# A two-layer decoder trunk in fp32: the down projections by a Winograd form of Strassen's algorithm, with weight sums on GpSimd

## The chip, the cores and the metric

The kernel runs on one core of a Trainium2 chip. Five engines work side by side, each in its own program order: TensorE (PE, matmuls), VectorE (DVE), ScalarE (ACT), GpSimd (POOL) and SyncE (SP, which issues DMAs). They meet only through semaphores. SBUF is the memory on the core, PSUM holds the sums of the matmuls in 8 banks of 128 partitions x 512 fp32, and DRAM is outside the core. The metric is the device time of one execution in microseconds.

## The reference, cut to what matters

There are 256 tokens, a model width of 2048, and two layers. Each layer is a mixer (sliding-window attention in layer 0, forgetting attention in layer 1) and then a SwiGLU network with 5632 hidden columns. All is fp32.

```
for i in range(DEPTH):                       # DEPTH = 2
    h = rmsnorm(x, g[0])
    y = attention(h)                         # two kinds
    x = x + rmsnorm(y, g[1])
    h = rmsnorm(x, g[2])
    gu = h @ w_gate_up                       # 2048 x 11264
    y = (silu(gate) * up) @ w_down           # 5632 x 2048: the down projection
    x = x + rmsnorm(y, g[3])
```

## The kernel before, in words

**Products in three parts.** TensorE takes the values in a rounded fp32 format (F32R), so each operand is split into a high part (the rounded value) and a low part (the rest). A product is three matmuls: high x high, high x low, low x high (`product`, L1336 to L1340). Each is 128x128 weights (the tokens' block) against 128x512 of the weight matrix, summed in a PSUM bank.

**The weights' way.** SP loads pairs of 128x512 weight tiles into `stage` (8 tiles). ACT rounds a tile into `ring_hi` (`round_tile`, L594 to L607), DVE writes the rest, `stage` minus `ring_hi`, into `ring_lo` (`rest_tile`, L808 to L817). Both rings have 24 tiles. Where the norm's gain is folded in (gate, up, q, k, v) ACT scales, and DVE uses a scalar_tensor_tensor (L817), else a tensor_tensor (L815).

**Units and steps.** The program is a row of units of 16 weight tiles. A unit has 32 steps: a step is one product, 3 matmuls, and each tile is used for both token blocks (t = 0, 1). While PE works through a unit, ACT and DVE prepare the next unit's tiles, one every second step. In what order each engine does its other work is written out by step numbers in tables at the top of the file.

**The SwiGLU network** works in 11 groups of 512 hidden columns. A group has three units: gate, up, down. After the up unit DVE makes `h_sb` = silu(gate) * up (L1061), turns it into `h_t` by 32x32 transposes (L1087, 32 instructions in a group), ACT rounds `h_t` into `h_hi` (L752), DVE makes `h_lo` (L1069). The down unit multiplies it with a 512 x 2048 block of `w_down`: 16 tiles x 2 token blocks = 32 products, 96 matmuls. After each of the 8 output chunks (2 token blocks x 4 column chunks) DVE adds the bank to `y_sb` in SBUF (`add_y`, L1106; L1103 copies in the first group). The residual `x_sb` (16 KB in each partition) lies in SBUF all the time. POOL does nothing in this network but a few small operations on the norms at its ends, and the load of the norm's gains.

**POOL's work elsewhere.** In the sliding-window layer POOL does the rotary embedding (L1220 to L1226: tensor_tensor of 128x64 and 128x128); in the forgetting layer it adds the mask to the bias (L1265, L1267: tensor_tensor 128x128, L1266: copy) and issues DMAs.

Of the kernel before, what the change touches and what calls it, by code (L numbers as in the profile page):

```python
# [7 lines left out]
F32 = mybir.dt.float32  # L8
# [35 lines left out]
LT = LOOP_UNITS * UT  # L44
# [6 lines left out]
U_FOX = U_FFN[0] + 3 * FG  # L51
U_FOX_OUT = U_FOX + FOX_UNITS
U_FFN[1] = U_FOX_OUT + NC_D
U_END = U_FFN[1] + 3 * FG
# [45 lines left out]
HIDDEN_TURNED = {(1, 17): (0, 0), (1, 19): (0, 1), (2, 1): (1, 0), (2, 3): (1, 1)}  # L100
HIDDEN_HI = {(1, 25): 0, (2, 5): 1}
HIDDEN_LO = {(1, 23): 0, (2, 5): 1}
# [32 lines left out]
def step_order(s, first=False):  # L135

    if first:
        return s // 4 % 2, s // 8 * 4 + s % 4
    return s // UT, s % UT

# [22 lines left out]
def build(nc, x, positions, norm_gains, swa_w_in, swa_sinks, swa_w_out,  # L163
          fox_w_in, fox_b_f, fox_w_out, ffn_w_gate_up, ffn_w_down, out):
    with ExitStack() as ctx:
# [40 lines left out]
        arena = sb("arena", [P, 51 * 1024 // 4])  # L206
# [22 lines left out]
        diag = at("diag", 40 * KB, [P, P])  # L229
        ssq_end = at("ssq_end", 41 * KB, [P, NC_D + 1])  # L230
# [18 lines left out]
        x_ps = [bank[b] for b in (6, 7, 4, 5)]  # L249

# [20 lines left out]
        x_sum = sem("x_sum")  # L271
        x_squared, pre_mean, pre_rstd = sem("x_squared"), sem("pre_mean"), sem("pre_rstd")
# [12 lines left out]

        cum_dram = nc.dram_tensor("cum_scratch", (NH, SEQ), F32, kind="Internal").ap()
# [4 lines left out]
        def weights(u, i, pr):  # L291
# [16 lines left out]
            if u < U_FOX or u >= U_FFN[1]:  # L308
                layer = 0 if u < U_FOX else 1
                g, part = divmod(u - U_FFN[layer], 3)  # L310
                g = g + i
                if part < 2:
                    return cols(ffn_w_gate_up[layer], g * CH + part * D_FF)
# [14 lines left out]
        def gain_row(u):  # L328

            if u < U_SWA_OUT:  # L330
                return 0
            if U_FOX <= u < U_FOX_OUT:
                return 4
            for layer in range(2):
                if U_FFN[layer] <= u < U_FFN[layer] + 3 * FG and (u - U_FFN[layer]) % 3 < 2:
                    return 4 * layer + 2
            return None
# [28 lines left out]

        def whole_program(loop, unit):

            def looped(u, n):
                with loop(n) as i:  # L370
                    for part in range(LOOP_UNITS):
# [6 lines left out]
            straight(U_SWA, U_FFN[0] + 3)  # L378
            looped(U_FFN[0] + 3, FG - 2)
            straight(U_FOX - 3, U_FOX + 3)  # L380
            looped(U_FOX + 3, NG - 2)
            straight(U_FOX_OUT - 3, U_FFN[1] + 3)
            looped(U_FFN[1] + 3, FG - 2)
            straight(U_END - 3, U_END)

        def ffn_part(u):

            for layer in range(2):
                if U_FFN[layer] <= u < U_FFN[layer] + 3 * FG:
                    return (layer, *divmod(u - U_FFN[layer], 3))  # L390
            return None
# [95 lines left out]
        def wait_transposed(eng, layer, g, i, t):  # L487
            if turned_on_pe(g, t):
                eng.wait_ge(ht_last, layer + 1)
            else:  # L490
                eng.wait_ge(ht_done, 2 * (layer * FG + g) - layer + t + 1 + 2 * i)

        def wait_swept(eng, u, i, t, n=0):
# [5 lines left out]
            elif t == 1:  # L499
                eng.wait_ge(tile_used, UT * u + (4 * (n + 1) if ffn and ffn[2] == 2 else UT) + LT * i)  # L500
            elif ffn is None:
                eng.wait_ge(proj_done, mixer_unit(u) + 1 + LOOP_UNITS * i)
            elif ffn[2] < 2:
                eng.wait_ge((gate_done, up_done)[ffn[2]], ffn[0] * FG + ffn[1] + 1 + i)
            else:
                eng.wait_ge(down_done, NC_D * (ffn[0] * FG + ffn[1]) + n + 1 + NC_D * i)
# [7 lines left out]
        def y_gain_count(b, t, q):  # L514

            k = NT * q + t if b % 2 else NC_D * t + q
            return 8 * (b - 1) + k + 1

# [6 lines left out]
        def _(sp):  # L525
# [26 lines left out]

            def unit(u, i):
                for pr in range(UT // PAIR):
                    if u == 0 and pr != 1:
# [3 lines left out]
                    if pair >= NSTAGE:  # L559

                        sp.wait_ge(raw_loaded[slot], 16)
                        sp.wait_ge(lo_ready, PAIR * (pair - NSTAGE + 1) + LT * i)
# [28 lines left out]
        def _(act):  # L591
            act.dma_start(gains_in[:, :], norm_gains.rearrange("l g (k p) -> (l g k) p", p=P)).then_inc(gains_loaded, 16)

            def round_tile(u, i, j):  # L594
# [3 lines left out]
                if j % PAIR == 0:  # L598
                    act.wait_ge(raw_loaded[pair % NSTAGE], loads_before(pair) + 16 * LT // STAGE * i)
                if n >= RING:  # L600
                    act.wait_ge(tile_used, n - RING + 1 + LT * i)
                row = gain_row(u)
                src = stage[:, n % STAGE, :]
                if row is None:
                    nc.scalar.activation(ring_hi[:, n % RING, :], src, ACT.Identity).then_inc(hi_ready, 1)  # L605
                else:
                    nc.scalar.activation(ring_hi[:, n % RING, :], src, ACT.Identity,  # L607
                                         scale=g_t[:, row * KT + j:row * KT + j + 1]).then_inc(hi_ready, 1)

# [92 lines left out]
            def unit(u, i):  # L702
                ffn = ffn_part(u)
                for s in range(STEPS):
# [33 lines left out]
                    if ffn:  # L738
                        layer, g, part = ffn
                        f = layer * FG + g  # L740
                        if part == 1 and s in (0, 2):
# [28 lines left out]
                    if s % 2 == 0 and u + 1 < U_END:  # L770
                        round_tile(u + 1, i, s // 2)

            def squares_of_y(b, t, n):

                f = (b // 2) * FG - 1
# [18 lines left out]
            for h in range(2):  # L794
                act.wait_ge(y_added, 8 * 2 * FG + h)
# [11 lines left out]
        def _(dve):  # L807
            def rest_tile(u, i, j):  # L808

                n = u * UT + j  # L810
                dve.wait_ge(hi_ready, n + 1 + LT * i)
                row = gain_row(u)
                src, hi, lo = stage[:, n % STAGE, :], ring_hi[:, n % RING, :].bitcast(F32), ring_lo[:, n % RING, :]
                if row is None:
                    nc.vector.tensor_tensor(lo, src, hi, ALU.subtract).then_inc(lo_ready, 1)  # L815
                else:
                    nc.vector.scalar_tensor_tensor(out=lo, in0=src, scalar=g_t[:, row * KT + j:row * KT + j + 1], in1=hi,  # L817
                                                   op0=ALU.mult, op1=ALU.subtract).then_inc(lo_ready, 1)

# [35 lines left out]
            def residual_sum(b, t, q):  # L855

                if q == 0:
                    dve.wait_ge(post_rstd, 2 * (b - 1) + t + 1)
                dve.wait_ge(y_gained, y_gain_count(b, t, q))
# [133 lines left out]
            def unit(u, i):  # L993
                ffn = ffn_part(u)
                for s in range(STEPS):
# [57 lines left out]
                    if ffn:  # L1053
                        layer, g, part = ffn
                        f = layer * FG + g
                        if (part, s) in ((1, 17), (2, 1)):

                            t = 0 if part == 1 else 1
                            dve.wait_ge(gate_read, 2 * f + t + 1 + 2 * i)
                            wait_swept(dve, u if part == 1 else u - 1, i, t)  # L1060
                            nc.vector.scalar_tensor_tensor(out=h_sb[:, t, :], in0=main[2 + t][:, :], scalar=pre_r[:, t:t + 1],  # L1061
                                                           in1=h_sb[:, t, :], op0=ALU.mult, op1=ALU.mult).then_inc(hidden, 1)
                        if (part, s) in HIDDEN_TURNED and not turned_on_pe(g, HIDDEN_TURNED[part, s][0]):
                            turn_hidden(layer, g, i, *HIDDEN_TURNED[part, s])
# [26 lines left out]
            def add_y(u, f, i, g, k):  # L1091
# [496 lines left out]
```

## Time and profile before

| | |
|---|---|
| median of 3 timed runs | 2106.15 us (2105.09 to 2106.24) |
| profiled execution, first to last instruction | 2104.5 us |
| PE, busy share of the span | 100% |
| DVE | 77% |
| ACT | 55% |
| POOL | 7% |

The profile page gives the profiled execution by its span alone. Matmuls overlap in the pipeline, so PE's busy time is a union: that PE is busy all the time doesn't say how close its matmuls follow. The number of matmuls in a stretch does. A group of instructions is a source line with an operation and the names of what it writes and reads; "busy, mean ns" is the sum and the mean duration of one, and a duration includes what the instruction waits for on its own data path once it has started.

### The profile page before, as it was taken

To read this page: it belongs to the slowest core of one execution; us is meant where nothing else is said; L and a number is where in the kernel's file an instruction comes from. 1 tells how busy PE (TensorE), PEld (TensorE's weight loads), DVE (VectorE), ACT (ScalarE), POOL (GpSimd) and SP (SyncE) were. 2 spreads that over 40 slices of the span, in tenths; PEclk is the share of its full clock that TensorE was granted. 3 is DMA by queue.
4 is the path that set the end of the run, shared out by engine and by line. 5 is a ranking of instruction groups with operands and counts; after the bars stand their busy time and mean duration, and the time that the engine had idled before them with its cause. 6 is when DMAs were issued, how large, how long until landed. Compare 5 with 4: busy or idle time off the path is not lost.

```text
span 2104.5 us, 32177 instructions
## 1 busy us (share of the span) xinstructions
PE 2094.2 (100%) x9603; PEld 1718.9 (82%) x9603; DVE 1615.4 (77%) x3299; ACT 1152.9 (55%) x2061; POOL 156.6 (7%) x311
## 2 busy tenths in 40 slices
PE   9999999999999999999999999999999999999998
PEld 7877888888888888888888887888888888888886
DVE  6798677887667776678898898577877668776686
ACT  7666565544455454555666555665544545445553
POOL 2110000000000000000152343000000000000000
PEclk9999999999999999999999999999999999999999
DMA  7699866665666655665687787756555665556662
GB/s 257 211 247 253 223 206 206 195 191 173 199 199 199 197 171 190 199 204 161 202 247 219 214 251 215 234 190 216 189 187 178 199 217 184 188 178 203 206 193 87
DMA packets 221564, 425.01 MB, mean 202 GB/s; under 512 B 15808, under 2 KB 25440, under 8 KB 220976
## 3 DMA queue, kind: packets, MB, share of 16 engines
q1 hardware_dynamic: 214528, 402.45, 61.6%
q0 software_dynamic: 6672, 21.31, 3.7%
q8 instruction: 37, 0.61, 0.1%
q10 hardware_dynamic: 288, 0.33, 0.1%
q14 instruction: 39, 0.32, 0.1%
HBM read 409.31 MB, written 14.71 MB: 201 GB/s over the span
## 4 chain that ended last, share of the span: by engine, by line
PE 97%; DMA 1%; issue 1%; SPq 1%; ACT 0%; POOL 0%; DVE 0%; POOLq 0%
PE bank L1338 31%; PE bank L1340 31%; PE bank L1339 31%; PE bank L1385 1%; PE bank L1410 1%; PE bank L1351 1%; DMA x_sb<-x 0%; DMA p_f<-first_scratch 0%; DMA stage<-swa_w_out 0%; PE bank L1368 0%; SPq L541 0%; SPq L566 0%; PE bank L1432 0%; PE bank L1429 0%; PE bank L1571 0%
## 5 line engine op out<-in xcount | busy, mean ns | idle before, releaser
L1338 PE MATMUL bank<-ring_hi,a_hi 128*128 128x512 f32 x2240 | 880.3, 393 | 0.5 <-DVE ring_lo L817 0.5
L1340 PE MATMUL bank<-ring_hi,a_lo 128*128 128x512 f32 x2240 | 873.1, 390 | 0.0
L1339 PE MATMUL bank<-ring_lo,a_hi 128*128 128x512 f32 x2240 | 872.8, 390 | 0.0
L607 ACT ACTIVATE ring_hi<-stage,g_t 128x512 fp32r<-128x512 f32 x992 | 661.2, 717 | 376.6 <-DMA stage<-ffn_w_gate_up 203.0
L817 DVE SCALAR_TENSOR_TENSOR ring_lo<-stage,g_t,ring_hi 128x512 fp32r<-128x512 f32 x992 | 708.5, 759 | 147.3 <-ACT ring_hi L607 144.9
L1338 PEld LDWEIGHTS bank<-ring_hi,a_hi 128*128 128x128 f32 x2240 | 420.9, 188 | 92.9 <-issue 5.9
L1340 PEld LDWEIGHTS bank<-ring_hi,a_lo 128*128 128x128 f32 x2240 | 420.8, 188 | 88.1
L1339 PEld LDWEIGHTS bank<-ring_lo,a_hi 128*128 128x128 f32 x2240 | 421.1, 188 | 84.7
L815 DVE TENSOR_TENSOR ring_lo<-stage,ring_hi 128x512 fp32r<-128x512 f32 x480 | 305.5, 687 | 139.9 <-ACT ring_hi L605 138.5
L605 ACT ACTIVATE ring_hi<-stage 128x512 fp32r<-128x512 f32 x480 | 278.4, 624 | 225.0 <-PE bank L1340 149.5
L1338 PE MATMUL bank<-ring_hi,h_hi 128*128 128x512 f32 x704 | 274.6, 390 | 0.0
L1340 PE MATMUL bank<-ring_hi,h_lo 128*128 128x512 f32 x704 | 274.2, 389 | 0.0
L1339 PE MATMUL bank<-ring_lo,h_hi 128*128 128x512 f32 x704 | 274.2, 389 | 0.0
L1087 DVE STREAM_TRANSPOSE h_t<-h_sb 32x128 f32<-32x128 f32 x672 | 203.5, 303 | 10.8
L1340 PEld LDWEIGHTS bank<-ring_hi,h_lo 128*128 128x128 f32 x704 | 132.2, 188 | 27.4
L1338 PEld LDWEIGHTS bank<-ring_hi,h_hi 128*128 128x128 f32 x704 | 132.3, 188 | 27.2
L1339 PEld LDWEIGHTS bank<-ring_lo,h_hi 128*128 128x128 f32 x704 | 132.3, 188 | 27.1
L1205 POOL TENSOR_TENSOR post_r<-post_ms,half_pow 128x1 f32<-128x1 f32 x8 | 7.6, 948 | 1491.6 <-DVE post_ms L844 1491.6
L1106 DVE TENSOR_TENSOR y_sb<-bank,y_sb 128x512 f32<-128x512 f32 x159 | 109.5, 688 | 11.6 <-PE bank L1340 10.8
L1061 DVE SCALAR_TENSOR_TENSOR h_sb<-bank,pre_r,h_sb 128x512 f32<-128x512 f32 x44 | 33.0, 749 | 108.8 <-PE bank L1340 108.8
L752 ACT ACTIVATE h_hi<-h_t 128x512 fp32r<-128x512 f32 x42 | 26.6, 633 | 125.7 <-DVE h_t L1087 125.7
L667 ACT ACTIVATE prob<-prob,neg_mx 128x129 f32<-128x129 f32 (+3 forms) x128 | 56.9, 447 | 39.6 <-DVE neg_mx L933 39.3
(148 smaller groups left out, 836.6 us busy)
## 6 DMA issues: line engine op xcount, KB each, us to landing
stage<-ffn_w_gate_up SPq DMA_DIRECT2D x352, 512.0 KB, 4.6
stage<-ffn_w_down SPq DMA_DIRECT2D x176, 512.0 KB, 5.5
stage<-fox_w_in SPq DMA_DIRECT2D x96, 512.0 KB, 4.7
stage<-swa_w_in SPq DMA_DIRECT2D x48, 512.0 KB, 4.7
stage<-swa_w_out SPq DMA_DIRECT2D x64, 256.0 KB, 6.2
stage<-fox_w_out SPq DMA_DIRECT2D x32, 512.0 KB, 5.5
first_scratch<-first_blocks SPq DMA_DIRECT2D x16, 384.0 KB, 5.4
p_f<-first_scratch SPq DMA_DIRECT2D x64, 96.0 KB, 3.9
```

Source lines behind the costliest of these rows:

```text
L605: nc.scalar.activation(ring_hi[:, n % RING, :], src, ACT.Identity).then_inc(hi_ready, 1)
L607: nc.scalar.activation(ring_hi[:, n % RING, :], src, ACT.Identity, scale=g_t[:, row * KT + j:row * KT + j + 1]).then_inc(hi_ready, 1)
L667: last = nc.scalar.activation(prob[:, b, cols], prob[:, b, cols], ACT.Exp, bias=neg_mx[:, j, t:t + 1], accum_out=den[:, j, t:t + 1])
L752: nc.scalar.activation(h_hi[:, :, tok(t)], hidden_transposed(g, t), ACT.Identity).then_inc(ht_hi, 1)
L815: nc.vector.tensor_tensor(lo, src, hi, ALU.subtract).then_inc(lo_ready, 1)
L817: nc.vector.scalar_tensor_tensor(out=lo, in0=src, scalar=g_t[:, row * KT + j:row * KT + j + 1], in1=hi, op0=ALU.mult, op1=ALU.subtract).th ...
L1061: nc.vector.scalar_tensor_tensor(out=h_sb[:, t, :], in0=main[2 + t][:, :], scalar=pre_r[:, t:t + 1], in1=h_sb[:, t, :], op0=ALU.mult, op1= ...
L1087: last = nc.vector.transpose(h_t[Q * b:Q * (b + 1), :, P * t + Q * a:P * t + Q * (a + 1)], src)
L1106: nc.vector.tensor_tensor(dst, main[n][:, :], dst, ALU.add).then_inc(y_added, 1)
L1338: nc.tensor.matmul(dst, hi_a, hi_w, start=start, stop=False)
L1339: nc.tensor.matmul(dst, hi_a, lo_w, start=False, stop=False)
L1340: return nc.tensor.matmul(dst, lo_a, hi_w, start=False, stop=stop)
```

## The change

All down products but those of the last of the 11 groups of a layer are computed by the Winograd form of Strassen's algorithm. The product of a group (256 tokens x 512) with half of its down block (512 x 1024) is cut into 2x2 blocks (128 tokens x 256, and 256 x 512) and takes 7 block products in place of 8. A block product is two weight tiles side by side, 6 matmuls. There are 20 such halves in a layer.

- The down units of these ten groups are gone. Their 7 block products (`down_pair`) are spread over the gate and the up unit of the next group, at steps 17, 19, 21, 23, 25, 27, 31 (gate) and 4, 8, ... 28 (up). A group thus has two units of 96 + 42 matmuls. In the first group of a layer the gate and the up unit are as before, and after the last group's up unit comes its down unit as before.
- The weight sums are made on POOL, four tensor_tensor of 128 x 1024 for a half (`sum_weights`), and two of the seven rests (T1, T4) as well. The other five rests are DVE's (`rest_pair`, 128 x 1024). ACT rounds all seven (`round_pair`). The sums of the hidden blocks are four tensor_tensor of 128 x 256 on POOL for a group (`sum_hidden`); ACT rounds them, DVE makes their rests (`sum_rests`).
- DVE adds each of the 7 products to `y_sb` from its bank (`add_pair`, 128x512), 14 in a group. Transposes are over both token blocks at once (`turn_group`, 16 of 32x256 in a group), the rest of the hidden block is one of 128x1024 (`hidden_rests`).
- The down weights are loaded into the place of `x_sb` (`down_w`, one buffer of 128 x 8 x 512). `x_sb` is stored to DRAM before the first half of a layer, and loaded back after the last (`save_x`, `load_x`, on POOL's queue).
- The ring has 16 fixed places for tiles and 4 x 2 for the block products' pairs. In the units with block products t changes every 4 steps (`step_order`).

```diff
+FFN_UNITS = 2 * FG + 1
...
-U_FOX = U_FFN[0] + 3 * FG
+U_FOX = U_FFN[0] + FFN_UNITS
+NPROD = 7
+B11, B21, T1, T2, B22, T3, T4 = range(NPROD)
+POOL_LO = (T1, T4)
+PRODUCT_STEPS = ((17, 19, 21, 23, 25, 27, 31), (4, 8, 12, 16, 20, 24, 28))
+PAIR_HI = ({18: (0, 4), 20: (0, 5), 22: (0, 6), 25: (1, 0), 27: (1, 1), 29: (1, 2)},
+           {0: (0, 3), 6: (0, 4), 10: (0, 5), 14: (0, 6), 18: (1, 0), 22: (1, 1), 26: (1, 2), 30: (1, 3)})
...
+            def load_down(u, i, second):
+                if q % NP_LAYER == 0:
+                    sp.wait_ge(x_saved, 16 * (layer + 1))
...
+            def round_pair(u, i, k):
+                wait_place(act, ("pair", p), i, u)
+                nc.scalar.activation(ring_hi[:, PLACE["pair", p]:PLACE["pair", p] + 2, :], pair_source(k), ACT.Identity).then_inc(pair_hi, 1)
...
+            def rest_pair(u, i, k):
+                dve.wait_ge(pair_hi, p + 1 + 4 * NPROD * i)
+                nc.vector.tensor_tensor(ring_lo[:, both, :], pair_source(k), ring_hi[:, both, :].bitcast(F32), ALU.subtract).then_inc(pair_lo, 1)
...
+            def add_pair(u, i, k):
+                nc.vector.tensor_tensor(dst, ps[:, :], dst, ALU.add).then_inc(pair_added, 1)
...
+            def sum_weights(q, i):
+                wait_loaded(0)
+                if q > 0:
+                    wait_rested(T4, q - 1)
+                nc.gpsimd.tensor_tensor(sums[0][:, :, :], b11, b12, ALU.add).then_inc(sums_made, 1)
+                wait_loaded(2)
+                pool.wait_ge(pair_lo, rested + DVE_LO.index(B11) + 1)
+                nc.gpsimd.tensor_tensor(sums[1][:, :, :], b22, b12, ALU.add).then_inc(sums_made, 1)
+                pool.wait_ge(sums_made, made + 1)
+                nc.gpsimd.tensor_tensor(sums[2][:, :, :], sums[0][:, :, :], b22, ALU.add).then_inc(sums_made, 1)
+                rest(T1)
+                pool.wait_ge(sums_made, made + 3)
+                wait_rested(T1, q)
+                nc.gpsimd.tensor_tensor(sums[0][:, :, :], sums[2][:, :, :], b21, ALU.add).then_inc(sums_made, 1)
+                if q % 2 == 0:
+                    sum_hidden(q, i)
+                rest(T4)
...
+            def down_pair(u, i, k):
+                for r in range(2):
+                    last = product(ps[:, :], a_h, a_l, ring_hi[:, slot, :], ring_lo[:, slot, :], k < 3 and r == 0, r == 1, True)
+                last.then_inc(pair_done, 1)
```

## Rows read from the trace of the kernel before

**Rows 1.** The page's first part: busy time and instructions of each engine.
```profile
PE 2094.2 (100%) x9603; PEld 1718.9 (82%) x9603; DVE 1615.4 (77%) x3299; ACT 1152.9 (55%) x2061; POOL 156.6 (7%) x311
```

**Rows 2.** Busy time by window: PE, PEld, DVE, ACT, POOL; clock, DMA share, GB/s.
```profile
300.00:365.28 65.28, 65.28 (x290) 54.10 (x289) 49.14 (x92) 32.84 (x52) 0.00 (x0) 1.00 0.62 198
2084.00:2104.40 20.40, 14.20 (x56) 10.03 (x54) 12.41 (x24) 4.80 (x14) 1.89 (x2) 0.88 0.29 103
```

**Rows 3.** Timeline of ACT, one instruction of three groups in turn: start, duration.
```profile
355.30 0.69 ACT L747 ACTIVATE h_sb<-bank,pre_r 128x512 f32<-128x512 f32 x1 [3.27 <-PE bank L1340]
420.57 0.69 ACT L747 ACTIVATE h_sb<-bank,pre_r 128x512 f32<-128x512 f32 x1 [3.38 <-PE bank L1340]
485.86 0.69 ACT L747 ACTIVATE h_sb<-bank,pre_r 128x512 f32<-128x512 f32 x1 [3.35 <-PE bank L1340]
```

**Rows 4.** The page's groups: count | busy, mean ns | idle before, releaser.
```profile
L1338 PE MATMUL bank<-ring_hi,h_hi 128*128 128x512 f32 x704 | 274.6, 390 | 0.0
L605 ACT ACTIVATE ring_hi<-stage 128x512 fp32r<-128x512 f32 x480 | 278.4, 624 | 225.0 <-PE bank L1340 149.5
```

**Rows 5.** Groups of DVE between 300 and 1000 us (the SwiGLU network of layer 0).
```profile
L817 DVE SCALAR_TENSOR_TENSOR ring_lo<-stage,g_t,ring_hi 128x512 fp32r<-128x512 f32 x339 | 238.5, 749 | 54.3 <-ACT ring_hi L607 54.0
L815 DVE TENSOR_TENSOR ring_lo<-stage,ring_hi 128x512 fp32r<-128x512 f32 x168 | 105.9, 687 | 45.9 <-ACT ring_hi L605 45.4
L1087 DVE STREAM_TRANSPOSE h_t<-h_sb 32x128 f32<-32x128 f32 x336 | 101.8, 303 | 5.4
L1106 DVE TENSOR_TENSOR y_sb<-bank,y_sb 128x512 f32<-128x512 f32 x80 | 55.1, 689 | 5.3 <-PE bank L1340 5.0
L1061 DVE SCALAR_TENSOR_TENSOR h_sb<-bank,pre_r,h_sb 128x512 f32<-128x512 f32 x22 | 16.5, 749 | 54.3 <-PE bank L1340 54.3
L1069 DVE TENSOR_TENSOR h_lo<-h_t,h_hi 128x512 fp32r<-128x512 f32 x21 | 14.4, 684 | 0.0
```

**Rows 6.** Groups of DVE over the whole span, two other shapes.
```profile
L877 DVE STREAM_TRANSPOSE k_t<-stg 32x256 f32<-32x256 f32 x64 | 27.9, 436 | 1.0
L952 DVE TENSOR_TENSOR a_lo<-bank,a_hi 128x256 fp32r<-128x256 f32 x8 | 3.0, 419 | 4.6 <-ACT a_hi L690 4.6
```

**Rows 7.** Single lines: duration in ns min/median/max, first and last start.
```profile
L1265 POOL TENSOR_TENSOR prob<-cum_b,mask x32: 456/474/1000, 1047.1 to 1288.0; 128x128 f32<-128x128 f32 x32
L1220 POOL TENSOR_TENSOR rope_tmp<-stg,rope_s x10: 322/362/875, 34.2 to 166.4; 128x64 f32<-128x64 f32 x10
L620 ACT ACTIVATE y_sb<-x_sb x6: 1907/1908/1909, 278.4 to 1393.4; 128x2048 f32<-128x2048 f32 x6
L928 DVE CUSTOM_DVE_ANT_0 prob<-bank,prob x64: 279/353/423, 1051.1 to 1301.0; 128x128 f32<-128x128 f32 x32, 128x256 f32<-128x256 f32 x32
```

**Rows 8.** Timeline 1280 to 1290 us, DVE, then POOL (first and last of six).
```profile
1285.94 0.38 DVE L952 TENSOR_TENSOR a_lo<-o_t,a_hi 128x256 fp32r<-128x256 f32 x1
1286.84 2.53 DVE L952 TENSOR_TENSOR a_lo<-o_t,a_hi 128x256 fp32r<-128x256 f32 x1
...
1286.91 0.48 POOL L1265 TENSOR_TENSOR prob<-cum_b,mask 128x128 f32<-128x128 f32 x1
...
1288.64 0.45 POOL L1267 TENSOR_TENSOR prob<-cum_b,mask 128x128 f32<-128x128 f32 x1
```

**Rows 9.** Timeline 34 to 40 us: DVE, and one of POOL's in it.
```profile
34.73 5.71 DVE L817 SCALAR_TENSOR_TENSOR ring_lo<-stage,g_t,ring_hi 128x512 fp32r<-128x512 f32 x7 [0.29 <-ACT ring_hi L607]
...
38.22 0.79 POOL L1224 TENSOR_TENSOR stg<-stg,rope_c 128x128 f32<-128x128 f32 x1
```

**Rows 10.** Timeline 1090 to 1110 us, DVE: POOL busy at first, idle at last.
```profile
1097.83 3.02 DVE L817 SCALAR_TENSOR_TENSOR ring_lo<-stage,g_t,ring_hi 128x512 fp32r<-128x512 f32 x3
...
1102.70 1.41 DVE L817 SCALAR_TENSOR_TENSOR ring_lo<-stage,g_t,ring_hi 128x512 fp32r<-128x512 f32 x2
```

**Rows 11.** Timeline of ACT: the squares of x at the start of the network.
```profile
284.40 1.91 ACT L620 ACTIVATE y_sb<-x_sb 128x2048 f32<-128x2048 f32 x1
```

More of the change, by code:

```diff
@@ L132, with ffn_index, pair_unit, pair_number @@
 OUT_GAIN = {84: (0, 0), 88: (1, 0), 92: (0, 1), 98: (1, 1), 102: (0, 2), 106: (1, 2)}
-def step_order(s, first=False):
-    if first:
+def ffn_index(u):
+    for layer in range(2):
+        if U_FFN[layer] <= u < U_FFN[layer] + FFN_UNITS:
+            return layer, u - U_FFN[layer]
+    return None
+def pair_unit(u):
+    f = ffn_index(u)
+    return f is not None and 2 <= f[1] < 2 * FG
+def pair_number(u):
+    layer, n = ffn_index(u)
+    return NP_LAYER * layer + n - 2
+def in_fours(u):
+    f = ffn_index(u)
+    return f is not None and 1 <= f[1] < 2 * FG - 1
@@ new lines, in pairs_rounded, with ring_places @@
+def pairs_rounded(u, s):
+    f = ffn_index(u)
+    if f is None or f[1] == 0 or s not in PAIR_HI[f[1] % 2]:
+        return []
+    later, k = PAIR_HI[f[1] % 2][s]
+    return [(u + later, k)] if pair_unit(u + later) else []
+def ring_places():
+    place, before, last = {}, {}, {}
+    n = 0
+    for u in range(U_END):
+        f = ffn_index(u)
+        fixed = f is not None and f[1] >= 2
+        if fixed and f[1] == 2:
+            first = n % RING
+        for j in range(UT):
+            slot = (first + j) % RING if fixed else n % RING
+            if not fixed:
+                n += 1
+            place[u, j] = slot
+            before[u, j] = last.get(slot)
+            last[slot] = ("tile", u * UT + j)
+        if pair_unit(u):
+            for k in range(NPROD):
+                p = NPROD * pair_number(u) + k
+                slot = (first + UT + 2 * (p % 4)) % RING
+                place["pair", p] = slot
+                before["pair", p] = last[slot + 1]
+                last[slot] = last[slot + 1] = ("pair", p)
+        if fixed and f[1] == 2 * FG:
+            n = first + UT
+    return place, before
@@ new lines, in turn_group @@
+            def turn_group(u, i, a):
+                layer, g, _ = ffn_part(u)
+                if a == 0:
+                    dve.wait_ge(hidden, 2 * (layer * FG + g - 1) + 2 + 4 * i)
+                    if pair_number(u) >= 2:
+                        dve.wait_ge(s_made, 2 * pair_number(u) + 8 * i)
+                for b in range(P // Q):
+                    src = h_sb[Q * a:Q * (a + 1), :, :].rearrange("p t (k b j) -> p t k b j", k=4, j=Q)[:, :, :, b, :]
+                    dst = h_t[Q * b:Q * (b + 1), :, :].rearrange("p k (t a i) -> p t k a i", t=NT, i=Q)[:, :, :, a, :]
+                    last = nc.vector.transpose(dst, src)
+                if a == P // Q - 1:
+                    last.then_inc(ht_done, 1)
@@ L1517, in unit @@
                     n_k = 4 if down else KT
[L1518 removed]
+                    last = product(dst[:, :], a_h[:, k, tok(t)], a_l[:, k, tok(t)], ring_hi[:, PLACE[tile], :], ring_lo[:, PLACE[tile], :],
                                    k == 0, k == n_k - 1)
```

386 lines of the change are left out of this document (306 added, 80 removed).

## The prediction

> **What bounds the kernel now.** I read the page's busy shares first, then the windows of the SwiGLU network, then DVE's groups in it, and last the timeline wherever DVE and POOL run together. The shares [rows 1] say PE 100%, DVE 77%, ACT 55%, POOL 7%. In the network the same instruction comes back every 65.28 us (420.57 - 355.30 = 65.27, 485.86 - 420.57 = 65.29) [rows 3]: that is one group. A group holds 288 product matmuls, so PE issues one every 65.28 / 288 = 226.7 ns; the 390 ns of one [rows 4] overlap. In that window PE is busy for all 65.28 us at clock 1.00, DVE for 49.14, ACT for 32.84, POOL for none [rows 2]. DVE's idle time there ends with ACT's rounding or with PE's bank [rows 5]: both follow PE. So PE sets the pace, and DVE has 16.1 us of slack in a group. The network is 2 x 11 groups of the kernel, the change touches 20 of them.
>
> **PE's part.** A group had 96 down matmuls and gets 2 x 7 x 6 = 84. That is 12 x 226.7 ns = 2.72 us less, a group of 62.56 us if PE stays the bound, and 20 x 2.72 = 54.4 us in all. Nothing on PE is added.
>
> **DVE's own work in a group**, by durations of rows 5 and 6:
> - rests of gate and up tiles: 32 x 0.749 = 24.0 us, as before.
> - rests of block products: 10 of 128x1024. No such size is in the trace. 256 columns take 0.419 [rows 6] and 512 take 0.687 [rows 5], so 1.05 ns a column and 1.22 us for 1024: 12.2 us, for 16 x 0.687 = 11.0 before. The bounds are 0.687 (if further columns were free) and 1.37 (twice 0.687).
> - additions to y: 14 x 0.689 = 9.6 us, for 8 x 0.689 = 5.5.
> - silu x up: 2 x 0.749 = 1.5, as before.
> - transposes: 16 of 32x256 at 0.436 = 7.0, for 32 x 0.303 = 9.7.
> - rest of the hidden block 1.22, and rests of its sums 2 x 0.687 = 1.4; before 2 x 0.684 = 1.4.
>
> This sums to 56.9 us, for 53.1 before. The 53.1 show as 49.14 busy [rows 2], because neighbours overlap by 4.0 us over 92 instructions, 0.043 each; 77 instructions give 3.3, so DVE needs 53.6 us of the 62.56. ACT rounds 14 pairs of 128x1024 in place of 16 tiles: with 0.624 for 512 [rows 4] and 1.91 for 2048 [rows 7], 0.84 ns a column, a pair is 1.05 us and 14 are 14.8 for 10.0 before; with the sums' rounding ACT stays near 40 us. SP's loads are the same bytes. By these alone PE would still be the bound.
>
> **POOL's work in a group**, which is new: 12 tensor_tensor of 128x1024 and 4 of 128x256. Rows 7 have 128 columns at 0.456 at the least (median 0.474) and 64 at 0.322, so 2.2 ns a column. Then 1024 columns take 0.46 + 896 x 0.0022 = 2.43 us, 256 take 0.74, and a group 12 x 2.43 + 4 x 0.74 = 32.1 us. Bounds for one of 1024: 0.46 (if columns were free) and 8 x 0.474 = 3.8. I take 2.43, since two rows give the slope. POOL has the time for it in 62.56 us. The Trainium skill, page "GPSIMD Engine Reference", section 3.1, has a tensor_tensor of 2048 fp32 columns at 4497 ns, an estimate of about 2.3 us for 1024; no row here shows either size.
>
> **What POOL does to DVE** is the term that decides. At 1286.84 a DVE tensor_tensor of 256 columns with both inputs in SBUF takes 2.53 us, where its neighbour takes 0.38. Beside it lie six POOL instructions without a gap, from 1286.91 to 1288.64 + 0.45 = 1289.09, which is 2.18 us, all at their undisturbed durations [rows 8]. DVE lost 2.53 - 0.42 = 2.11 us of these 2.18: it waited for all of them. Three rests take 3.02 us beside POOL's, where two alone take 1.41 [rows 10], so three would take 2.08. The wait goes both ways: POOL's 128-column tensor_tensor takes 0.79 beside DVE's rests [rows 9], and up to 1.00 [rows 7]. DVE's operations with one input in PSUM show none of it: L928 ranges from 0.279 to 0.423 over two shapes, also beside POOL's [rows 7]. The Trainium skill, page "SBUF — State Buffer", section "Who interferes with whom", has this as a rule: a DVE instruction with two SBUF inputs contends with a GpSimd instruction that reads SBUF, and whoever has the shared port keeps it for the whole instruction. By that rule, the trace agrees: 2.11 of 2.18 us. It speaks against this change, whose gain was worked out above as if the engines were free of each other.
>
> Of DVE's 56.9 us, those with two SBUF inputs are 24.0 + 12.2 + 1.2 + 1.4 = 38.8 us. Only the additions, transposes and silu x up, 18.1 us, can run while POOL computes. DVE works in order, and after nearly each addition (0.689) comes a rest. The transposes, 7 us in one stretch (steps 2 to 8 of the gate unit), lie where POOL waits for their result or has at most one operation. So of a POOL operation of 2.43 us DVE hides a fraction of one addition and stands still for the rest. Bounds of DVE's loss: the share of rows 8, 97% of 32.1 = 31 us; and the share of rows 9, where seven rests take 5.71 us for 0.75 + 6 x 0.66 = 4.7 undisturbed [rows 10], so 1.0 us lost beside seven small POOL operations of some 2.8 us, 35%, that is 11 us. Long operations are nearer to rows 8, because what isn't lost in rows 9 is the fixed part of a short one. With 18.1 of 56.9 us free of the port I take 78%: 25 us. Then DVE needs 53.6 + 25 = 78.6 us in a group, more than PE's 62.56 and than the 65.28 of before. DVE is the bound, and PE waits for `ring_lo`. The slack that costs nothing now is 62.56 - 53.6 = 9 us; from a loss of 65.28 - 53.6 = 11.7 us on (36% of POOL's time) the kernel is slower than before.
>
> 20 x (78.6 - 65.28) = +266 us.
>
> **Waits at the ends.** The store of x waits for the squares, which end at 284.40 + 1.91 = 286.3 [rows 11]. It moves 2.1 MB, 10.6 us at 198 GB/s [rows 2] beside the weights, and the first down block, as large, comes behind it, at about 308. ACT asks for it at step 18 of the first up unit, about 289 + 18 x 0.68 = 301, and what is queued behind it on ACT are the next unit's tiles from the seventh on, and behind these DVE's rests and PE. With six tiles ready PE can go on for some 8 us. I take 2.5 us for a layer, from 0 to 10, 5 in all. SP stands still meanwhile too, but `stage` holds 8 tiles. The way back, x and the gains (3 MB, about 16 us), is asked for after the last rests, about step 18 of the last up unit; x is wanted at step 17 of the down unit, some 26 us later: hidden.
>
> **Sum.** Span 2104.5 + 266 + 5 = 2375.5; the timed median lies 1.65 us above this span, so 2377 us.
>
> **Rivals.**
> 1. *PE stays the bound.* POOL's operations fall into DVE's slack, or the long ones hold DVE for less than the short ones suggest: 2106.15 - 54.4 + 5 = 2057 us. For it: 9 us of slack, and rows 9 with 35%. Against it: 38.8 - 2 us of DVE and even 26 us of POOL on one port are 63 us in a group of 62.56, before any order is looked at. It decides from a loss under 9 us. Chance 0.14, and 0.03 for what comes out between it and no change, 0.03 for no change.
> 2. *DVE is the bound but hides half:* a loss of 16 us, a group of 69.6 us, +86 + 5: 2197 us. For it: POOL's operations wait for each other's semaphores and for ACT, and let DVE in between. Chance 0.15.
> 3. *PE's clock falls as well.* At the end PE is busy 14.2 of 20.4 us and the granted clock is 0.88 of 2.4 GHz, so part of it was at 1.2 [rows 2]. If PE's gaps did that in a quarter of the groups, each would take 2 x 62.56 = 125 us: 5 x (125 - 78.6) = +232, 2609 us. Against it: DVE's stops are some 2.4 us, between bursts of matmuls, and PE would be busy 80%. Chance 0.04.
>
> **Numbers.** The forecast has 0.61. Its own range is a loss of 19 to 31 us: 72.6 to 84.7 us a group, 2258 to 2500. The range that holds 8 in 10 leaves out rival 1 and the far ends, and takes in rival 2: 2130 to 2480. What a measurement of this kernel tells from no change is about 0.2%, 4 us. Faster 0.17, same 0.03, slower 0.80.
>
> **What would show it.** The period of a group in the windows: near 79 us, PE busy about 80%, DVE over 95%. DVE's rests (L817's successor) with a mean well above 0.749, and `rest_pair`'s above 1.22 and up to 3.6, while the additions stay at 0.69 and the transposes at 0.44. POOL's operations of 1024 columns at 2.4 us at the least, and often longer. PE's idle time released by `ring_lo`. It would be wrong if the period is near 62.6, or if the rests keep their durations beside POOL's, or if PE waits for POOL's sums instead.

## The result, and the profile after

The changed kernel takes 2344.3 us (median of 4 runs, 2342.72 to 2344.4) for 2105.93 of the kernel before: a ratio of 1.113, 95% interval 1.1115 to 1.1146. The forecast was 2377. The span is 2342.6 us, 238.1 more than before, where 271 were forecast.

First the page of the changed kernel: busy time of each engine, then groups (count | busy, mean ns | idle before, releaser). They answer to [rows 1, 4, 5].

```profile
PE 2130.2 (91%) x9363; PEld 1720.3 (73%) x9363; DVE 2094.3 (89%) x2999; ACT 1264.3 (54%) x2041; POOL 916.3 (39%) x635
...
L1694 PE MATMUL bank<-ring_hi,h_hi 128*128 128x512 f32 x304 | 141.2, 465 | 198.9 <-DVE y_sb L1083 149.7
L1034 DVE TENSOR_TENSOR ring_lo<-down_w,ring_hi 128x1024 fp32r<-128x1024 f32 x120 | 254.3, 2119 | 1.8 <-ACT ring_hi L793 1.7
```

PE has 240 matmuls less and is no longer busy all the time; DVE has 300 instructions less and is busy for 479 us more. The windows of the SwiGLU network (columns as in [rows 2]), first 550 us, then one group of it:

```profile
400.00:950.00 550.00, 483.66 (x2000) 390.95 (x1999) 527.50 (x565) 274.72 (x366) 270.51 (x116) 0.95 0.51 165
584.37:660.19 75.82, 66.63 (x278) 53.85 (x277) 73.54 (x78) 38.57 (x53) 38.03 (x17) 0.95 0.52 166
```

DVE is busy 96% of the time, PE 88%, POOL 49%. The bound has moved from PE to DVE. The period is again that of one ACT instruction, the silu of a gate tile, in the timeline of ACT; it answers to [rows 3]:

```profile
507.23 0.66 ACT L946 ACTIVATE h_sb<-bank,pre_r 128x512 f32<-128x512 f32 x1
...
584.37 0.66 ACT L946 ACTIVATE h_sb<-bank,pre_r 128x512 f32<-128x512 f32 x1
...
660.19 0.67 ACT L946 ACTIVATE h_sb<-bank,pre_r 128x512 f32<-128x512 f32 x1
```

77.14 and 75.82 us; over the four periods from 507.23 to 813.05 the mean is 76.5, and over the 18 inner periods of both layers 76.2, for 65.28 before. (A layer has 10 periods from its first silu to that of its last group; the first one is counted apart below.) What has grown is in the groups of DVE between 400 and 950 us, which answer to [rows 5]:

```profile
L1024 DVE SCALAR_TENSOR_TENSOR ring_lo<-stage,g_t,ring_hi 128x512 fp32r<-128x512 f32 x230 | 274.2, 1209 | 2.7 <-ACT ring_hi L780 2.5
L1034 DVE TENSOR_TENSOR ring_lo<-down_w,ring_hi 128x1024 fp32r<-128x1024 f32 x42 | 89.0, 2119 | 0.0
L1046 DVE STREAM_TRANSPOSE h_t<-h_sb 32x256 f32<-32x256 f32 x128 | 55.8, 436 | 3.0
L1085 DVE TENSOR_TENSOR y_sb<-bank,y_sb 128x512 f32<-128x512 f32 x70 | 47.6, 681 | 7.5 <-PE bank L1696 7.2
L1034 DVE TENSOR_TENSOR ring_lo<-sums,ring_hi 128x1024 fp32r<-128x1024 f32 x29 | 35.1, 1210 | 0.0
...
L1054 DVE TENSOR_TENSOR h_lo<-h_t,h_hi 128x1024 fp32r<-128x1024 f32 x8 | 12.4, 1548 | 9.3 <-ACT h_hi L802 9.3
```

The rests of gate and up tiles take 1.209 us in place of 0.749, the rests of `down_w` 2.119 where the same instruction on `sums` takes 1.210. These are means of two kinds, told apart by the start and end of each instruction in the trace: the 107 of the 230 rests of L1024 that lie beside a POOL operation take 1.748 us, the other 123 take 0.740; of the rests of `down_w`, 21 lie beside one and take 3.026, 21 don't and take 1.211. None of the 29 rests of `sums` lies beside one. Additions (one input in PSUM) stay at 0.68, also the 28 of L1083, all of which lie beside POOL operations. No transpose does in this window; they are put to the test in experiment 5. POOL in the same window:

```profile
L1590 POOL TENSOR_TENSOR ring_lo<-sums,ring_hi 128x1024 fp32r<-128x1024 f32 x28 | 79.2, 2829 | 140.7 <-ACT ring_hi L793 140.7
L1601 POOL TENSOR_TENSOR sums<-sums,down_w 128x1024 f32<-128x1024 f32 x14 | 43.3, 3090 | 0.0
```

The timeline shows how it happens. DVE first, then POOL, same stretch (start, duration):

```profile
582.93 2.83 DVE L1034 TENSOR_TENSOR ring_lo<-down_w,ring_hi 128x1024 fp32r<-128x1024 f32 x1
585.69 2.82 DVE L1024 SCALAR_TENSOR_TENSOR ring_lo<-stage,g_t,ring_hi 128x512 fp32r<-128x512 f32 x1
588.43 0.67 DVE L1083 TENSOR_TENSOR y_sb<-y_sb,bank 128x512 f32<-128x512 f32 x1
589.03 2.25 DVE L1024 SCALAR_TENSOR_TENSOR ring_lo<-stage,g_t,ring_hi 128x512 fp32r<-128x512 f32 x1
...
595.13 3.39 DVE L1024 SCALAR_TENSOR_TENSOR ring_lo<-stage,g_t,ring_hi 128x512 fp32r<-128x512 f32 x5
```

```profile
581.83 2.85 POOL L1599 TENSOR_TENSOR sums<-down_w 128x1024 f32<-128x1024 f32 x1 [1.16 <-DVE ring_lo L1034]
584.64 3.32 POOL L1601 TENSOR_TENSOR sums<-sums,down_w 128x1024 f32<-128x1024 f32 x1
587.92 2.81 POOL L1590 TENSOR_TENSOR ring_lo<-sums,ring_hi 128x1024 fp32r<-128x1024 f32 x1
590.81 2.71 POOL L1605 TENSOR_TENSOR sums<-sums,down_w 128x1024 f32<-128x1024 f32 x1
...
606.52 2.47 POOL L1590 TENSOR_TENSOR ring_lo<-sums,ring_hi 128x1024 fp32r<-128x1024 f32 x1 [12.99 <-ACT ring_hi L793]
```

Four POOL operations stand nearly back to back from 581.83 to 593.52. In them DVE gets through about one rest for each of POOL's: the rest that starts at 585.69 ends at 588.51, just behind POOL's end at 587.96. The addition in between takes its usual 0.67. Once POOL is done, at 595.13, five rests take 3.39 us together. The loss is mutual: POOL's 1024 columns take 2.47 us with little beside them (2.39 at the least, at 302.20 us, with DVE idle) and 2.7 to 3.3 here.

### The profile page after: what moved, and what is told of

It is laid out like the page before. It is cut to its first block and busy times, and to the rows that moved or that the text cites. A ratio compares the mean times of both kernels' runs of the same rounds, so it can differ in the third digit from the quotient of the medians.

```text
span 2342.6 us, 32002 instructions
## 1 busy us (share of the span) xinstructions
PE 2130.2 (91%) x9363; PEld 1720.3 (73%) x9363; DVE 2094.3 (89%) x2999; ACT 1264.3 (54%) x2041; POOL 916.3 (39%) x635
## 5 line engine op out<-in xcount | busy, mean ns | idle before, releaser
L1024 DVE SCALAR_TENSOR_TENSOR ring_lo<-stage,g_t,ring_hi 128x512 fp32r<-128x512 f32 x992 | 1020.1, 1054 | 72.7 <-ACT ring_hi L780 70.8
L1590 POOL TENSOR_TENSOR ring_lo<-sums,ring_hi 128x1024 fp32r<-128x1024 f32 x80 | 225.9, 2824 | 407.3 <-ACT ring_hi L793 407.3
L793 ACT ACTIVATE ring_hi<-sums 128x1024 fp32r<-128x1024 f32 x160 | 169.9, 1062 | 352.9 <-PE bank L1696 352.3
L1694 PE MATMUL bank<-ring_hi,h_hi 128*128 128x512 f32 x304 | 141.2, 465 | 198.9 <-DVE y_sb L1083 149.7
L1034 DVE TENSOR_TENSOR ring_lo<-down_w,ring_hi 128x1024 fp32r<-128x1024 f32 x120 | 254.3, 2119 | 1.8 <-ACT ring_hi L793 1.7
L1046 DVE STREAM_TRANSPOSE h_t<-h_sb 32x256 f32<-32x256 f32 x320 | 139.6, 436 | 7.0
L1022 DVE TENSOR_TENSOR ring_lo<-stage,ring_hi 128x512 fp32r<-128x512 f32 x160 | 104.1, 686 | 42.3 <-ACT ring_hi L778 41.8
L778 ACT ACTIVATE ring_hi<-stage 128x512 fp32r<-128x512 f32 x160 | 94.8, 624 | 83.2 <-DMA stage<-swa_w_out 36.5
L1696 PE MATMUL bank<-ring_hi,h_lo 128*128 128x512 f32 x304 | 136.0, 447 | 0.0
L1695 PE MATMUL bank<-ring_lo,h_hi 128*128 128x512 f32 x304 | 134.9, 444 | 0.0
```

The source lines that it names most:

```text
L793: nc.scalar.activation(ring_hi[:, PLACE["pair", p]:PLACE["pair", p] + 2, :], pair_source(k), ACT.Identity).then_inc(pair_hi, 1)
L1034: nc.vector.tensor_tensor(ring_lo[:, both, :], pair_source(k), ring_hi[:, both, :].bitcast(F32), ALU.subtract).then_inc(pair_lo, 1)
L1046: last = nc.vector.transpose(dst, src)
L1590: nc.gpsimd.tensor_tensor(ring_lo[:, both, :], pair_source(k), ring_hi[:, both, :].bitcast(F32), ALU.subtract).then_inc(pair_lo_pool, 1)
L1694: nc.tensor.matmul(dst, hi_a, hi_w, start=start, stop=False, skip_group_check=goes_on)
L1695: nc.tensor.matmul(dst, hi_a, lo_w, start=False, stop=False, skip_group_check=goes_on)
```

## The experiments

Theory A is the prediction's: POOL's operations that read SBUF stop DVE's operations with two SBUF inputs, and DVE is the bound. The rivals, B and C in the expectations, look for the time elsewhere, above all in the changed order of work and in what DVE itself has to do. Times are medians of 4 runs (10 in experiment 6), and ratios are to the kernel before on the same chip (2106.32 us for the first four kernels, 2105.83 for the last four).

**1. POOL's two rests go to DVE; the weight sums stay on POOL.**

```diff
-POOL_LO = (T1, T4)
+POOL_LO = ()
```

> The changed kernel, but the rests of T1 and T4 go from GpSimd to VectorE as well (POOL_LO is empty); nothing is left out. Theory A (the shared way into SBUF: a GpSimd operation of 1024 columns stops VectorE's two-input operations): VectorE's own work grows from 53.6 to 58.4 us a group (4 x 1.21), GpSimd's falls from 32.1 to 22.4, and at the share measured (21.1 of 32.1, 0.66) VectorE loses 14.8 in place of 21.1; with the 1.8 us of idle a group is 75.0 us and the time about 2315 us, slightly faster. Theory B (GpSimd's operations cost VectorE nothing, VectorE is the bound by its own work): 4.8 us more in each of 20 groups, 2440 us. Theory C (GpSimd's chain of sums is late and PE waits for it): the chain loses four operations a group, time falls to about 2106 - 54 + 15 = 2067 us.

Measured: 2291.35 us, ratio 1.088 (1.0865 to 1.0902), period 73.6 us. DVE has 4.9 us more of its own in a group, POOL some 10 us less, and the kernel is 53 us faster. The direction that B expects (2440) is refuted, and so is C, which expects 2067. A has the direction, and its size (2315) is off by 24 us: DVE loses 32 x (0.954 - 0.743) + 6 x (2.095 - 1.219) + 0.3 = 12.3 us in a group here, where A expects 14.8.

**2. The same, with POOL's sums written but not read.** Each tensor_tensor of a sum works on its first column alone, and a memset fills the rest of the destination. The sums are left out of what is computed; every wait, rest and product is there.

```diff
+            def fill(dst, a, b, op):
+                nc.gpsimd.tensor_tensor(dst[:, :, 0:1], a[:, :, 0:1], b[:, :, 0:1], op)
+                return nc.gpsimd.memset(dst[:, :, 1:], 1.0)
-                nc.gpsimd.tensor_tensor(sums[0][:, :, :], b11, b12, ALU.add).then_inc(sums_made, 1)
+                fill(sums[0][:, :, :], b11, b12, ALU.add).then_inc(sums_made, 1)
...
```

> As the kernel before it (all rests on VectorE), and GpSimd's twelve sums a group are not computed: a tensor_tensor of the first column of each row block, and a memset for the other columns, so that GpSimd writes as much and reads nearly nothing. VectorE's own work is 58.4 us a group as there. Theory A, if it is the reading that stops VectorE: no loss, 58.4 is less than PE's 62.56, PE is the bound, a group is 62.6 us and the time about 2344 - 20 x 13.9 = 2066 us; if writing stops it as well, about 1 us for each of 8 operations, at most 65 us a group and 2115 us. Theory B (VectorE's own work is the bound): as the kernel before it, over 2300 us.

Measured: 2094.1 us, ratio 0.994 (0.9924 to 0.9957), period 63.9 us. The window of 550 us, and two of DVE's groups in it:

```profile
400.00:950.00 550.00, 541.63 (x2382) 446.06 (x2381) 491.20 (x702) 329.08 (x440) 126.44 (x202) 1.00 0.61 197
```

```profile
L1024 DVE SCALAR_TENSOR_TENSOR ring_lo<-stage,g_t,ring_hi 128x512 fp32r<-128x512 f32 x269 | 195.8, 743 | 0.2
...
L1034 DVE TENSOR_TENSOR ring_lo<-down_w,ring_hi 128x1024 fp32r<-128x1024 f32 x51 | 62.2, 1219 | 3.7 <-ACT ring_hi L793 3.6
```

The rests are back at 0.743 and 1.219 us, though POOL still writes all the same bytes, and the schedule is the one of experiment 1. So the schedule alone costs no 250 us, and B (over 2300) is refuted. But it isn't free: the time is 42 us above 2106 - 54.4, what PE's matmuls alone would give, and 28 above A's 2066. That it also lies under A's 2115, for a POOL whose writes stop DVE too, says little; the durations of the rests decide between the two. The 42 us are taken up below.

**3. Sums and rests all on DVE.** The four sums of a half and those of the hidden block are DVE's, at steps of the gate and up units; POOL does nothing in the network.

```diff
+SUM_STEPS = ({24: 0, 27: 1, 28: 2, 31: 3}, {16: 0, 20: 1, 21: 2, 28: 3})
...
+                    nc.vector.tensor_tensor(sums[0][:, :, :], b11, b12, ALU.add).then_inc(sums_made, 1)
...
```

> All sums and all rests go on VectorE, in place of GpSimd, at steps next to where their inputs are ready; nothing is left out. VectorE's own work is then 53.6 + 4 x 1.21 + 8 x 1.21 + 4 x 0.42 = 69.8 us a group, and GpSimd does nothing in the groups. Theory A: no loss, with 1.8 us of idle 71.6 us a group, 2344 - 20 x 4.9 = 2247 us: faster than the changed kernel, though VectorE does 16 us more in each group, and slower than before. Theory B: 16.2 us more in each of 20 groups, 2668 us. Theory C: between 2070 and 2250 us.

Measured: 2222.46 us, ratio 1.055 (1.0536 to 1.0571), period 70.4 us. A expects 2247 and B 2668; C's 2070 to 2250 holds the result as well, so this time alone doesn't rule C out. DVE's rests do: they are back at 0.744 and 1.218 us, and DVE is busy for 96% of the window. Against experiment 1, DVE has 8 x 1.22 + 4 x 0.42 = 11.4 us more of its own in a group and loses 12.3 us less, so the work itself is nearly even. Most of the 3.2 us by which the group is shorter is idle time of DVE, 4.7 us there and 2.8 here. One group of DVE, and the window:

```profile
L1372 DVE TENSOR_TENSOR sums<-down_w 128x1024 f32<-128x1024 f32 x16 | 19.6, 1226 | 2.1
```

```profile
400.00:950.00 550.00, 510.18 (x2155) 416.20 (x2156) 528.36 (x719) 301.80 (x407) 0.00 (x0) 0.96 0.56 179
```

**4 and 5. The kernel before, with idle work on POOL.** 12 or 24 tensor_tensor of 128x1024 in each of ten groups of a layer, which read `ident` and write a buffer that nobody reads, each let go by the count of DVE's rests, so that they lie evenly. Nothing else of the kernel before is changed, neither products nor schedule.

```diff
+                        for k in range(24 * (FG - 1)):
+                            pool.wait_ge(lo_ready, UT * (U_FFN[layer] + 1) + 2 * (k + 1))
+                            pool.wait_ge(worked, 24 * (FG - 1) * layer + 1 * k)
+                            tile = ident[:, :].unsqueeze(1).to_broadcast([P, 8, P])
+                            nc.gpsimd.tensor_tensor(idle_work[:, :, :], tile, tile, ALU.add).then_inc(worked, 1)
```

> The kernel before, with twelve GpSimd operations in each of the first ten groups of a layer that nobody waits for: tensor_tensor of 128x1024, reading ident, writing a place that nothing else uses, one after each fourth rest of a tile. Nothing is left out. Theory A: VectorE needs 49.1 us a group and loses 12 x 2.2 x 0.8 = 21, 70 us, more than PE's 65.28: with a little idle about 71 us a group, 2106 + 20 x 5.7 = 2220 us. Theory B: no change, 2106 us, since nothing waits for these operations and VectorE has 16 us of slack.

Measured with 12: 2117.6 us, ratio 1.005 (1.0037 to 1.0071). My expectation missed by 100 us, and the time taken alone is nearer to the rival's. The groups of DVE and the window say why:

```profile
L818 DVE SCALAR_TENSOR_TENSOR ring_lo<-stage,g_t,ring_hi 128x512 fp32r<-128x512 f32 x278 | 271.3, 1028 | 2.3 <-ACT ring_hi L608 2.1
L816 DVE TENSOR_TENSOR ring_lo<-stage,ring_hi 128x512 fp32r<-128x512 f32 x130 | 117.3, 954 | 10.1 <-ACT ring_hi L606 9.4
```

```profile
400.00:950.00 550.00, 549.06 (x2414) 452.20 (x2413) 520.65 (x763) 277.62 (x441) 215.01 (x98) 1.00 0.63 194
```

The rests do grow, by 0.279 and 0.266 us: 32 x 0.279 + 16 x 0.266 = 13.2 us in a group. But DVE had 16.1 us of slack there, and 13.2 fill it to 95% busy without passing it. The expectation had taken 21 us of loss. So the time said nothing against A; the run was too weak. Doubling the work had to show.

> As before_plus_12 with 24 idle operations of 1024 columns a group, one after each second rest; nothing is left out. Theory A: with twelve, VectorE's durations grew by 13.2 us a group (1.1 each) and filled its slack without passing it (PE 65.3 to 65.6 us a group). With 24 there is no slack left, so each costs 1.1 to 2.2: VectorE needs 49.1 + 26 = 75 us at the least and 49.1 + 24 x 1.5 = 85 in the middle, 2106 + 20 x 15 = about 2400 us, from 2300 to 2520. Theory B (the twelve cost next to nothing because GpSimd and VectorE hardly hinder each other): twice 11 us more, 2130 us.

Measured with 24: 2429.6 us, ratio 1.154 (1.152 to 1.1558), period 81.7 us; A expects about 2400 in 2300 to 2520, B 2130.

```profile
L818 DVE SCALAR_TENSOR_TENSOR ring_lo<-stage,g_t,ring_hi 128x512 fp32r<-128x512 f32 x223 | 298.5, 1391 | 0.1
L816 DVE TENSOR_TENSOR ring_lo<-stage,ring_hi 128x512 fp32r<-128x512 f32 x102 | 128.1, 1314 | 0.3
L1088 DVE STREAM_TRANSPOSE h_t<-h_sb 32x128 f32<-32x128 f32 x208 | 63.0, 303 | 3.3
L1107 DVE TENSOR_TENSOR y_sb<-bank,y_sb 128x512 f32<-128x512 f32 x56 | 38.1, 680 | 0.2
```

```profile
400.00:950.00 550.00, 465.23 (x1960) 373.68 (x1961) 546.07 (x616) 221.51 (x352) 369.45 (x163) 0.94 0.53 155
```

DVE loses 32 x 0.642 + 16 x 0.626 + 2 x 0.848 (`h_lo`, 1.533 us) = 32.3 us in a group. Less the 16.1 of slack that is 16.2; the period grew by 81.7 - 65.28 = 16.4. With 12 the loss is under the slack, and the 11 us that the kernel grew by are 0.6 us for each of the 20 groups. So cost is loss less slack in both runs, to within 0.6 us a group. The transposes stay at 0.303 us here, and 65 of the 208 lie beside POOL operations.

**6. The same time on POOL, without reading.** The 24 tensor_tensor are 24 pairs of memset of 128x1024.

```diff
-                            nc.gpsimd.tensor_tensor(idle_work[:, :, :], tile, tile, ALU.add).then_inc(worked, 1)
+                            nc.gpsimd.memset(idle_work[:, :, :], 1.0).then_inc(worked, 1)
...
```

> As before_plus_24, but each idle operation is two memsets of 1024 columns one after the other, about 1.0 us each: GpSimd is busy for nearly as long, writes twice as much and reads nothing. If GpSimd's reading is what stops VectorE: VectorE's rests keep 0.749 and 0.687, 2106 us. If writing or being busy stops it as well: 48 memsets of 1 us, as before_plus_24, 2300 us or more.

Measured: 2105.36 us, ratio 1.000 (0.999 to 1.0009).

```profile
400.00:950.00 550.00, 550.00 (x2428) 455.54 (x2427) 407.83 (x760) 277.77 (x440) 368.92 (x387) 1.00 0.62 194
```

And the kernel before in the same window:

```profile
400.00:950.00 550.00, 550.00 (x2428) 455.75 (x2427) 407.91 (x761) 277.83 (x441) 0.00 (x0) 1.00 0.61 194
```

POOL is busy for 368.92 us, as in experiment 5 (369.45), and DVE for 407.83, as before (407.91). Being busy and writing cost nothing; reading costs 324 us.

**7 and 8. The store of x earlier.** In the changed kernel SP waits for the store of `x_sb` before it loads the first down block, as forecast; the waits of SP from 280 to 335 us:

```profile
SPq L723 <- DMA x_scratch<-x_sb: 9.0, 1, 9.0
```

Here the store is issued as soon as x is new, not after its squares and its transposes, in the kernel with the sums on POOL (7) and in that of experiment 3 (8).

```diff
+                    sp.wait_ge(x_squared, NT * NC_D + NT * (2 * layer + 1))
+                    sp.wait_ge(xt_done, NT * NC_D * (2 * layer + 2))
...
-                pool.wait_ge(x_squared, NT * NC_D + NT * b)
-                pool.wait_ge(xt_done, NT * NC_D * (b + 1))
+                pool.wait_ge(x_new, 2 * NC_D * b)
```

> The changed kernel, with the store of x issued as soon as x is made (its squares and transposes then only have to end before the down weights come, which SyncE waits for); nothing is left out. SyncE's wait for the store was 17.1 us in two, and the first group of a layer took about 10 us more than its matmuls. Theory A: the store is the late link at the ends, 5 to 9 us a layer come back, 2330 us. Rival (VectorE would have been late there anyway): no change, 2344 us.

> All sums and rests on VectorE, and the early store; nothing is left out. By theory A the two savings add: 2222 less 10 to 18 us, 2208 us, still slower than before (2106), because VectorE's own 69.8 us a group is more than 65.28. Rival: the saving of the early store vanishes, 2222 us.

Measured: 2344.47 us, ratio 1.113 (1.1112 to 1.115), and 2222.36, ratio 1.055 (1.0532 to 1.0567); both as without the edit. So the expectations of theory A (2330 and 2208) missed by 14 us each, and the rival held. The store goes out at 270.9 us in place of 286.6, and SP's wait for it is gone. Yet PE's gap ahead of the first product with `h_hi` stays, in (7):

```profile
333.98 0.80 PE L1696 MATMUL bank<-ring_hi,h_hi 128*128 128x512 f32 x1 [11.80 <-DVE h_lo L1056]
```

and in the changed kernel, where the second fence has DVE ahead of it:

```profile
335.16 0.80 PE L1694 MATMUL bank<-ring_hi,h_hi 128*128 128x512 f32 x1 [11.81 <-DVE h_lo L1054]
```

```profile
323.66 1.78 DVE L1046 STREAM_TRANSPOSE h_t<-h_sb 32x256 f32<-32x256 f32 x4
...
328.82 3.59 DVE L1046 STREAM_TRANSPOSE h_t<-h_sb 32x256 f32<-32x256 f32 x8
333.53 1.57 DVE L1054 TENSOR_TENSOR h_lo<-h_t,h_hi 128x1024 fp32r<-128x1024 f32 x1 [1.12 <-ACT h_hi L802]
```

The store wasn't what PE waited for; the chain from the end of the last silu x up at 323.6 to the first product (16 transposes, ACT's rounding of 1.06 us, `h_lo`) is 11.5 us long, and DVE makes two rests in it. When that chain starts does depend on POOL. The last silu x up in the changed kernel, then the same one and the first product in experiment 2:

```profile
322.88 0.74 DVE L1363 SCALAR_TENSOR_TENSOR h_sb<-bank,pre_r,h_sb 128x512 f32<-128x512 f32 x1
```

```profile
316.97 0.74 DVE L1363 SCALAR_TENSOR_TENSOR h_sb<-bank,pre_r,h_sb 128x512 f32<-128x512 f32 x1
...
328.90 0.80 PE L1698 MATMUL bank<-ring_hi,h_hi 128*128 128x512 f32 x1 [5.93 <-DVE h_lo L1054]
```

Where POOL doesn't read, DVE comes to it 5.9 us earlier, and PE's gap is 5.9 us in place of 11.8. The other half of the gap stays without any contention.

## Why the prediction was right, point by point

**The mechanism was right.** DVE became the bound because POOL reads SBUF. Three pairs of runs show it from three sides: reading or not in the changed schedule (1 and 2: 2291 and 2094), reading or not in the schedule of before (5 and 6: 2430 and 2105), and the work moved off POOL (3: 2222 for 2344). The Trainium skill, page "SBUF — State Buffer", section "Who interferes with whom", makes the same distinction, that a GpSimd instruction which only writes doesn't contend; by that rule, experiment 6 agrees: no change of DVE's 407.9 us.

**How close the time is, is in part luck.** Two errors work against each other: the 20 groups cost 20 x 10.96 = 219 us where 266 stood, and the ends 19 where 5 stood. Together they leave 238 for 271.

**PE's part.** It issues 276 matmuls a group. Where next to nothing reads beside DVE (experiment 2), the period is 63.9 us and not 62.56; PE's only wait in the window is that of the product for `h_lo`, 8.4 us in 8 groups. That is 20 x 1.34 = 27 of the 42 us; the other 15 lie at the ends. Of the 54.4 us, 12 come out in that schedule.

**DVE's own work.** The 128x1024 rest was taken at 1.22 and is 1.21 to 1.22; the transposes at 0.436 and are 0.436; additions 0.681 for 0.689. DVE is busy 527.50 / 550 x 76.2 = 73.1 us in a group; less the loss below that is 52.4, for 53.6 forecast.

**POOL's durations.** 2.39 us undisturbed for 1024 columns, 2.43 forecast. The working has a slip: 0.456 and 0.322 us for 128 and 64 columns give 2.1 ns a column and not 2.2, and so 2.34 us. The idle operations of experiments 4 and 5, with a broadcast of `ident` as both inputs, take 1.89 us undisturbed.

**DVE's loss, the term that was mis-sized.** With the undisturbed durations of experiment 2, 32 x (1.209 - 0.743) + 6 x (2.119 - 1.219) + (1.548 - 1.22) = 14.9 + 5.4 + 0.3 = 20.6 us in a group, where 25 stood; 64% of the 32.1 us, where I took 78% between bounds of 35 and 97. The four rests of `sums` in a group aren't touched at all (1.210), since none of them lies beside a POOL operation. The share is not a constant either. Per POOL operation of 1024 columns DVE loses 1.7 us here, 1.5 in experiment 1, 1.34 with 24 idle ones in a group (2.28 us each beside DVE) and 1.10 with 12 (2.19). In the last, where DVE has slack, POOL's operations have a DVE instruction with two SBUF inputs beside them for 78% of their time, with 24 for 89%. That goes the way of the difference, but no run separates it from the rest.

**The period.** 52.4 + 20.6 + 3.1 us in which DVE is idle = 76.1, and 76.2 was measured; 78.6 was forecast with no idle time. The idle time of DVE ends with PE's bank (7.2 us in the 550) and ACT's `h_hi` (9.3): DVE waits once a group for the rounding behind its own transposes.

**Which wait PE shows.** I expected `ring_lo`. PE's largest wait on the page ends with DVE's addition L1083, 149.7 us, the next with `h_lo`. In the timeline above the addition of 588.43 frees the bank for the product at 589.16; it was itself late behind the two long rests. It is the same cause at another semaphore, but that step named the wrong one. The waits of PE over the whole span:

```profile
PE bank L1694 <- DVE y_sb L1083: 149.7, 40, 4.6
PE bank L1694 <- DVE h_lo L1054: 49.2, 20, 11.8
...
PE bank L1694 <- DVE ring_lo L1024: 0.9, 1, 0.9
```

PE was to be busy for about 80% of the window, and is for 88%.

**The ends.** Forecast 5 us, by the store of x. Of the 238.1 us, 18 inner periods give 18 x 10.9 = 197 and the first period of each layer 20.6 in the two (75.4 and 74.4 for 64.6 before, from the silu of the second token block to the next). From the last group's silu to the next layer and to the end it is 10.6 and 11.3 us more. But half of the last block products moved there (42 matmuls, 9.5 us each time), out of the first period, in which PE has only 234 matmuls or 53.0 us. So the ends cost some 19 us over 20 periods of 10.96, and the place of the loss is the first group of a layer, with its 11.8 us gap of PE. Experiments 7 and 8 show that the store isn't its cause. By experiment 2 half of the gap is DVE's loss beside POOL once more. The other half, 5.9 us, is there with no contention; that it is the chain behind the transposes was read from the timeline, and not tried by an experiment. So the step that took the ends at 5 us had the wrong cause, and the size came out nearly four times as large.

**The rivals.** Rival 1, PE stays the bound, 2057 us: refuted, and its price was too low as well, as without contention it is 2094 (in experiment 2, whose DVE has 4.9 us more of its own in a group). Rival 2, a loss of half (16 us): the loss, 20.6, lies midway between it and the forecast's 25. It is DVE's idle time, which neither has, that brings the time (2344) nearer to the forecast (2377) than to the rival (2197). Rival 3, PE's clock: the granted clock is 0.95 in the window, so a small part of the time is at the lower level of 1.2 GHz, as in experiment 5 (0.94). DVE is busy 96% in the same window, so PE's clock doesn't set the pace; no run took it away.

**Left open.** Half of the halves by block products, with all sums on DVE, would by the rows of experiment 3 leave DVE near 60 us a group, under PE's 64. That is an estimate. In experiment 2 all the halves together bring 12 us, so half of them would bring some 6; it wasn't tried. So no version here computes the whole and beats the kernel before.

## What to carry to other kernels

Before work goes to GpSimd, ask of each operation whether it reads SBUF, and how much of VectorE's work has two inputs there. Its cost is what VectorE loses less the slack that VectorE has. Here a 1024-column operation cost VectorE 1.22 us when VectorE made it. On GpSimd it cost VectorE 1.7 us on average with sums and rests there, and 1.5 with the sums alone, so nothing was gained by moving it. An experiment with idle work must be large enough to pass the slack, or it shows nothing. And when an algorithm saves multiplications, first list what its operand sums and rests cost on the engine that prepares the operands; here 2.7 us of PE were bought with 4 us of DVE even before the sums.

## What the runs showed that I had not expected

- A GpSimd that is busy 67% of the time with memsets (0.956 us for 128x1024) left every DVE group at its duration to within 1 ns (0.749, 0.303, 0.689), the other engines' windows too.
- GpSimd reads can take 13.2 us of a group from DVE and the kernel slows by only 0.5%: DVE's busy share rises from 74% to 95% in the window while PE stays at 99.8%. A busy share of 95% can thus hold a fifth of waiting within instructions.
- A tensor_tensor of two columns on POOL that reads `down_w` took 0.627 to 0.678 us on average in experiment 2. With DVE idle (at 301.90 and 307.93 us) it took 0.19 and 0.20, and one on `h_t` that started with `h_lo` (1.23 us on DVE, at 327.6) took 1.28: short POOL operations, too, wait for DVE's.
